# A hybrid decoder step with a 32-expert MoE: the experts' tokens picked out by one-hot products instead of indirect DMA

## What is computed

```python
h = _rmsnorm(x, norm_ffn)                       # 320 rows of 1024
logits = h @ w_router + b_router                # 32 experts
top_v, top_e = lax.top_k(logits, 4); gate = softmax(top_v)
# for each expert e, with the rows xe of h that chose it:
gu = xe @ w_gu[e] + b_gu[e]                     # 1024 x 2048
gt, up = jnp.split(gu, 2, axis=-1)              # clamped at 7
act = gt * sigmoid(1.702 * gt) * (up + 1.0)
out = act @ w_dn[e] + b_dn[e]                   # 1024 x 1024
# y[token] = sum over its four experts of gate * out
```

## Time and profile before

| | before |
|---|---|
| median of 3 runs | 1393.08 us (1392.92 to 1396.97) |
| the profiled execution, its own time | 1394.72 us |
| span in the profile | 1393.0 us |
| PE busy | 1274.7 us (92%) |
| DVE, ACT, POOL busy | 446.9, 238.9, 113.2 us |
| moved by DMA | 480.87 MB |

### The profile page before, as it was taken

How to read it: one execution, slowest core, us unless ns; L and a number is a source line. 1 busy time by engine, 2 the same in 40 slices (tenths; PEclk the granted TensorE clock), 3 DMA queues, 4 the chain that set the end, 5 groups by cost and what they waited for, 6 DMA issues and landing times.

```text
span 1393.0 us, 14359 instructions
## 1 busy us (share of the span) xinstructions
PE 1274.7 (92%) x5899; PEld 578.1 (41%) x5899; DVE 446.9 (32%) x793; ACT 238.9 (17%) x343; POOL 113.2 (8%) x140
## 2 busy tenths in 40 slices
PE   6999899999999999999999999999988877778881
PEld 5665677676463333333333333333332222223220
DVE  1697211121265331312222223322242222332216
ACT  3201343330121110111111111101121111111101
POOL 0110100000000100001100100001101100000100
PEclk9999999999999999999999999999999999999995
DMA  9614602734779999999999999999999999999994
GB/s 338 235 61 141 246 1 86 277 110 193 286 283 395 421 425 425 426 426 427 424 426 426 427 424 425 426 427 425 423 427 426 425 424 425 426 426 425 426 374 152
DMA packets 63366, 480.87 MB, mean 345 GB/s; under 512 B 11831, under 2 KB 11959, under 8 KB 38569
## 3 DMA queue, kind: packets, MB, share of 16 engines
q1 hardware_dynamic: 51327, 464.60, 80.8%
q0 software_dynamic: 9584, 10.37, 2.1%
q10 hardware_dynamic: 2362, 4.56, 0.9%
HBM read 479.83 MB, written 22.35 MB: 361 GB/s over the span
## 4 chain that ended last, share of the span: by engine, by line
PE 72%; DMA 24%; DVE 1%; ACT 1%; issue 1%; SPq 0%; POOL 0%; POOLq 0%; DVEq 0%
PE PS L1629 28%; PE PS L1290 15%; PE PS L1660 14%; DMA XX<-in_w_dn 12%; DMA XX<-in_w_gu 9%; PE PS L1236 4%; PE PS L1450 4%; PE PS L1492 3%; PE PS L1314 2%; DMA arena<-y_rows 1%; DMA ring<-in_w_in 1%; DMA arena<-h_rows,arena 1%; DMA y_rows<-arena 1%; PE PS L1368 0%; PE PS L1535 0%
## 5 line engine op out<-in xcount | busy, mean ns | idle before, releaser
L1629 PE MATMUL PS<-ring,arena 128*64 128x512 f32 x1840 | 412.3, 599 | 30.5 <-DMA ring<-in_w_gu 25.4
L1151 DVE TENSOR_TENSOR arena<-PS,XX 128x1024 f32<-128x1024 f32 x32 | 39.2, 1225 | 656.4 <-PE PS L1629 656.4
L1629 PEld LDWEIGHTS PS<-ring,arena 128*64 128x64 f32 x1840 | 130.5, 138 | 287.2 <-issue 285.2
L1290 PE MATMUL PS<-arena,ring 128*128 128x320 f32 x768 | 214.7, 437 | 3.1 <-DMA ring<-in_w_in 3.1
L1290 PEld LDWEIGHTS PS<-arena,ring 128*128 128x128 f32 x768 | 145.8, 192 | 63.7 <-issue 7.0
L1660 PE MATMUL PS<-ring,arena 128*64 128x512 f32 x656 | 148.2, 602 | 11.1 <-DMA ring<-in_w_dn 9.0
L790 ACT ACTIVATE arena<-arena 128x1024 f32<-128x1024 f32 x32 | 33.8, 1058 | 625.2 <-DVE arena L1154 625.1
L521 POOL DMA_INDIRECT y_rows<-arena x64 | 63.9, 998 | 823.9 <-ACT arena L781 814.1
L1629 PE MATMUL PS<-arena 128*64 128x512 f32 x432 | 97.7, 603 | 11.0 <-DMA arena<-in_w_gu 11.0
L1660 PE MATMUL PS<-arena 128*64 128x512 f32 x384 | 85.3, 596 | 5.3 <-DMA arena<-in_w_dn 5.3
L1236 PEld LDWEIGHTS PS<-ident,arena 128*128 128x128 f32 (+4 forms) x596 | 65.4, 143 | 58.5 <-issue 48.4
(11 more groups left out here) (190 smaller groups left out, 757.5 us busy)
## 6 DMA issues: line engine op xcount, KB each, us to landing
ring<-in_w_gu SPq DMA_DIRECT2D x95, 2048.0 KB, 29.5
ring<-in_w_dn SPq DMA_DIRECT2D x33, 2048.0 KB, 31.6
arena<-in_w_gu SPq DMA_DIRECT2D x22, 2048.0 KB, 29.4
arena<-in_w_dn SPq DMA_DIRECT2D x20, 2048.0 KB, 28.5
ring<-in_w_in SPq DMA_DIRECT2D x12, 2048.0 KB, 12.2
XX<-in_w_dn SPq DMA_DIRECT2D x11, 2048.0 KB
XX<-in_w_gu SPq DMA_DIRECT2D x10, 2048.0 KB
ring<-in_w_mem_kv SPq DMA_DIRECT2D x2, 2048.0 KB, 20.1
```

The costliest lines, as they stand in the source:

```text
L1151: nc.vector.tensor_tensor(gbuf[:], PS[:, 0:2, :], g_bias, ALU.add).then_inc(main["g_added"], 1)
L1290: last = mm(PS[:, j % 2, 0:T], w[:, k, m * P:(m + 1) * P], hT[:, k, :], start=k == 0, stop=k == KT - 1)
L1629: last = mm(PS[64 * h:64 * h + 64, 2 * g + b, :], tokens[:, k, :], (spare[kk] if m == BONUS else moe_ring(m, 2)[:, kk]) [:, g * D + h * 51 ...
```

## The change

The indirect fetch is gone: no `h_rows`, no `gather`, no `TG`, no `XG`. For every expert DVE's new `take` makes a one-hot `taken` (three row tiles x 128 slots, two buffers in turn) by comparing `R` with a row of numbers, `iota_s` or, for odd experts, the reversed `iota_b`, as `order` did for expert 0 alone. PE's new `take_tokens` stands where `turn_tokens` stood and multiplies it with `XN` in SBUF, as `first_tokens` did: 8 x 3 products instead of 8 transposes. The table has one column per expert. `XN` now has to stay whole through the loop, so `spread` (the bias rows by `stream_shuffle`, now two instructions of 512 columns), the gates `GD` and the loads of `b_dn` leave it, and `XX` is one row tile larger with `low` for small things. `turn_gates`, the copy `GT` and the two `b_dn` loads move behind the loop. The pieces of the diff below come in the order SP, POOL, ACT, DVE, PE, behind the one on the places in SBUF.

```diff
-    XX = sb("XX", [P, 2 * TT, D])
-    X, XN = XX[:, 0:TT, :], XX[:, TT:2 * TT, :]
+    XX = sb("XX", [P, 2 * TT + 1, D])
+    low, X, XN = XX[:, 0, :], XX[:, 1:TT + 1, :], XX[:, TT + 1:2 * TT + 1, :]
...
-    entries = view(16352, TT, TOPK, 2, NE)
+    entries = view(16352, TT, TOPK, NE)
-    XG = [view(15328, D), view(18400, D)]
+    taken = view(15328, 2, TT, WIN)
-    spread = XN[:, 2, :].rearrange("p (g n) -> p g n", g=2)
+    spread = [view(14816, 512), view(18400, 512)]
...
     # SP, ahead of the first load into LATE
                 sp.wait_ge(x_kept, 48)
-                sp.wait_ge(h_out, 48)
                 sp.wait_ge(main["xt_turned"], 1)
...
     # POOL
         def window(v):
-            pool.wait_ge(main["tg_ready"], v + 1)
-            if v:
-                gather(v, 0)
-            gather(v, 1)
             pool.wait_ge(main["zi_ready"], v + 1)
-            for e in range(2, NE):
-                gather(v, e)
-                if e >= 3:
-                    scatter(v, e - 3)
-            for e in range(NE - 3, NE):
+            for e in range(NE):
                 scatter(v, e)
...
     # ACT
         def keep_rows(tt):
-            rows = h_rows[tt * P:tt * P + ROWS[tt], :]
-            act.dma_start(rows, XN[0:ROWS[tt], tt, :]).then_inc(h_out, 16)
             act.dma_start(x_keep[tt * P:tt * P + ROWS[tt], :], X[0:ROWS[tt], tt, :]).then_inc(x_kept, 16)
...
-        for h in range(2):
-            act.dma_start(bdn[NE * h:NE * (h + 1), :], a["b_dn"][0][:, 512 * h:512 * (h + 1)]).then_inc(bdn_in, 16)
         act.wait_ge(cnt_ready, 1)
         most = act.value_load(maxi[0:1, 0:1], min_val=0, max_val=T)
         window(0)
...
+        act.wait_ge(gt_done, 1)
+        for h in range(2):
+            act.dma_start(bdn[NE * h:NE * (h + 1), :], a["b_dn"][0][:, 512 * h:512 * (h + 1)]).then_inc(bdn_in, 16)
+        nc.scalar.activation(GT[0:2 * NE, :], PS[0:2 * NE, 7, 0:T], ACT.Copy).then_inc(gt_ready, 1)
...
     # DVE
+        def take(v, e):
+            if NE * v + e > 1:
+                dve.wait_ge(main["xt_turned"], NE * v + e - 1)
+            for tt in range(TT):
+                r = ROWS[tt]
+                last = nc.vector.tensor_scalar(taken[0:r, e % 2, tt, :], (iota_b if e % 2 else iota_s)[0:r, :],
+                                               1024.0 + 512.0 * e + WIN * v, R[0:r, tt, e:e + 1], ALU.add, ALU.is_equal)
+            last.then_inc(main["taken_ready"], 1)
+
         fetch_list(0)
+        take(0, 1)
...
             for e in range(NE):
                 n = NE * v + e + 1
-                nc.vector.stream_shuffle(spread, bias[:], mask=[e] * 32).then_inc(main["spread_ready"], 1)
+                for g in range(2):
+                    last = nc.vector.stream_shuffle(spread[g], bias[:, g, :],
+                                                    mask=[e] * 32)
+                last.then_inc(main["spread_ready"], 1)
...
                     .then_inc(main["act_ready"], 1)
+                if e + 2 < NE:
+                    take(v, e + 2)
...
     # PE
-        def turn_tokens(v, e):
-            pe.wait_ge(main[f"gathered{e % 2}"], 16 * ((NE // 2) * v + e // 2 + e % 2))
-            rows = XG[e % 2]
-            if NE * v + max(e - 1, 0):
+        def take_tokens(v, e):
+            n = NE * v + e
+            pe.wait_ge(main["taken_ready"], n)
+            if n > 1:
                 pe.wait_ge(main["actT_ready"], NE * v + max(e - 1, 0))
+
             for k in range(KT):
-                last = tr(PS[:, 6 + k // 4, (k % 4) * WIN:(k % 4 + 1) * WIN], rows[:, k * P:(k + 1) * P])
+                for tt in range(TT):
+                    r = ROWS[tt]
+                    last = mm(PS[:, 6 + k // 4, (k % 4) * WIN:(k % 4 + 1) * WIN], XN[0:r, tt, k * P:(k + 1) * P],
+                              taken[0:r, e % 2, tt, :], start=tt == 0 and k % 4 == 0, stop=tt == TT - 1 and k % 4 == 3)
             last.then_inc(main["xt_turned"], 1)
```

More of the change, by code:

```diff
@@ L264, in program @@
     first_done, wr_ready = sem("first_done"), sem("wr_ready")
-    nffn_in, bias_in, h_out = (sem(s) for s in ("nffn_in", "bias_in", "h_out"))
+    nffn_in, bias_in = (sem(s) for s in ("nffn_in", "bias_in"))
     gates_ready, summed, x_kept, x_back = (sem(s) for s in ("gates_ready", "summed", "x_kept", "x_back"))
@@ L270, in program @@
     fin_in, fin_out = sem("fin_in"), sem("fin_out")
-    names = ("chunk_used", "spread_ready", "g_added", "u_clipped", "gathered0", "gathered1", "xt_turned", "xT_half", "xT_ready", "gu_done", "g_ready", "gu_read", "sig_done",
+    names = ("chunk_used", "spread_ready", "g_added", "u_clipped", "taken_ready", "xt_turned", "xT_half", "xT_ready", "gu_done", "g_ready", "gu_read", "sig_done",
              "prod", "act_ready", "ta_done", "actT_ready", "dn_done", "zs_ready", "scattered",
-             "shifted", "listed", "table_done", "tg_ready", "dest_ready", "moved", "zi_ready")
+             "shifted", "listed", "table_done", "dest_ready", "moved", "zi_ready")
     main = {s: sem(s) for s in names}
     bonus_in = sem("bonus_in")
-    h_rows = nc.dram_tensor("h_rows", (T, D), F32, kind="Internal").ap()
     x_keep = nc.dram_tensor("x_keep", (T, D), F32, kind="Internal").ap()
@@ L1135, in _ @@
             nc.vector.tensor_scalar(gates[0:r, tt, :], gsel[0:r, tt, :], gden[0:r, tt:tt + 1], None, ALU.mult)
-            if tt == 0:
-                dve.wait_ge(h_out, 48)
-                dve.wait_ge(main["xt_turned"], 1)
             for h in range(2):
@@ L1144, in window @@
         def window(v):
+            if v:
+                take(v, 0)
+                take(v, 1)
             for e in range(NE):
                 n = NE * v + e + 1
-                nc.vector.stream_shuffle(spread, bias[:], mask=[e] * 32).then_inc(main["spread_ready"], 1)
+                for g in range(2):
+                    last = nc.vector.stream_shuffle(spread[g], bias[:, g, :],
+                                                    mask=[e] * 32)
+                last.then_inc(main["spread_ready"], 1)
                 dve.wait_ge(main["spread_ready"], n)
                 dve.wait_ge(main["gu_done"], n)
-                g_bias, u_bias = (spread[:, i:i + 1, :].to_broadcast([P, 2, 512]) for i in range(2))
+                g_bias, u_bias = (spread[i][:, None, :].to_broadcast([P, 2, 512]) for i in range(2))
                 nc.vector.tensor_tensor(gbuf[:], PS[:, 0:2, :], g_bias, ALU.add).then_inc(main["g_added"], 1)
@@ L1549, in table_part @@
             for j in range(TOPK):
-                last = mm(PS[:, 7, 0:2 * NE], slots[0:r, tt, j, :], entries[0:r, tt, j].rearrange("p x e -> p (x e)"),
+                last = mm(PS[:, 7, 0:NE], slots[0:r, tt, j, :], entries[0:r, tt, j, :],
                           start=tt == 0 and j == 0, stop=tt == TT - 1 and j == TOPK - 1)
@@ L1694, in window @@
             if v:
-                turn_tokens(v, 0)
+                take_tokens(v, 0)
             for e in range(NE):
@@ L1706, in window @@
                 if e + 1 < NE:
-                    turn_tokens(v, e + 1)
-                elif v == 0:
-                    turn_gates()
+                    take_tokens(v, e + 1)
                 if e:
@@ L1714, in window @@
                     down(v, e - 1)
-                if v == 0 and e == NE - 1:
-                    pe.wait_ge(gt_ready, 1)
                 if e:
@@ L1742, in _ @@
         pe.nop()
+        turn_gates()
         for tt in range(TT):
```

46 lines of the change are left out of this document (13 added, 33 removed).

## The result

| | before | after |
|---|---|---|
| median | 1393.0 us (4 runs) | 1540.47 us (4 runs, 1539.65 to 1541.42) |
| ratio to before | | 1.1046, 95% interval 1.1032 to 1.106 |
| span in the profile | 1393.0 us | 1537.9 us |
| PE busy | 1274.7 us (92%) | 1490.6 us (97%) |
| moved by DMA | 480.87 MB | 474.60 MB |

147 us slower, where 71 were forecast, and far outside the range. The direction and the bound came out as written, and every term within 3 us but one, the price of the products.

What follows compares the result with a forecast made beforehand. Before, the weight stream bounds the experts, with PE equally full early; after, PE bounds the loop. Net PE work 153.2 less 79.1 idle gives +74.1, clock -1, end -2: +71 us, 1465.7 profiled, 1464 median; range 1450 to 1478.

Steps and rivals of the forecast that it cites:

- The price of the products: PE in the loop: 48 records at 0.125 us, 6.0 us an expert (5.9 to 6.2), net 4.98, in 31 turns 154.4 us.
- The idle time and the bound: PE behind expert 21: all 79.1 us of idle time are filled and PE becomes the bound of the whole loop.
- a lead that runs out: Weight ring behind the last expert with two blocks: its lead just lasts or falls short, adding 0 to 5 us.
- The first fetch: PE before expert 1's tokens: the wait of 1.19 us for the indirect DMA goes, gain 1.2 us.
- DMA: Weight stream: dropped fetches are worth 12 us to a stream that bounds, nothing to one that waits for PE.
- DVE: DVE in each turn: three comparisons, 0.7 to 0.9 us, and a bias spread in two parts, all hidden.
- The end: Behind the loop: between -4.3 and +2 us, taken as -2, and -1 for the clock in expert 31's `down`.
- rival 1: Loop behind expert 21: products hide in PE's idle time and the lighter stream makes it faster, 1381 us; 3%.
- Rival 2: Products in the loop: cheaper between long streams, 0.1 us a record, but not hidden, 1437 us; 6%.
- C: Follow-up theory on the products: records are slow because of the long streams around them, whatever their order; 8.4 us, 1540 us.
- Rival 3: Products in the loop: each costs four transposes, 12.3 us an expert, 1659 us; 1%.
- Rival 4: PE in each turn: a new wait for DVE or ACT, or a lower clock, 0.5 us a turn, 1480 us; 8%.

## Why the prediction was wrong, point by point

- **The price of the products: this is the step that failed.** "I take 0.125: 6.0 us an expert, bounds 5.9 and 6.2." It measured 8.45. Two things lay behind it. The 0.125 was a group's span divided by its count, and so held the 0.19 us of the group's edges and, in the 24, one change of height; the pace itself is 0.112. And `first_tokens` has the row tile outermost, which I named as the same shape without looking at the order in which the shapes follow each other. The two errors have opposite signs: without changes of height an expert would be 5.55, the fifteen changes make it 8.45. The bounds came from two rows of one and the same order, so they couldn't bound it.
- **The idle time and the bound: right.** Every microsecond of it filled, PE busy throughout, no wait on a chunk in the loop. With 8.45 in the place of 6.0 the working gives 1420.5 + 76.0 = 1496.5 for the turn of expert 31's activations; it is at 1496.80. The few microseconds for a lead that runs out were nothing at this price; with the row tile outermost and 5.75 us, where PE's own work alone would end at 1412.7, the turn is at 1420.63, so there they were 8.
- **The first fetch: right.** The products start behind `move_dest` with no wait, at 430.13 where the transposes started at 431.16:

```profile
429.56 0.64 PE L1544 MATMUL PS<-arena,ident 128*64 128x16 f32 x16
430.13 4.18 PE L1587 MATMUL PS<-arena,XX 128*128 128x128 f32 x23
```

- **DMA: right**, 11 us in a stream that binds, nothing here.
- **DVE: right.** The three comparisons take 0.66 us, behind the last step of an expert, and 22 us of waiting for gate/up follow:

```profile
522.44 0.66 DVE L1100 TENSOR_SCALAR arena<-iota_b,arena 128x128 f32<-128x128 f32 x3
...
545.97 1.23 DVE L1134 TENSOR_TENSOR arena<-PS,arena 128x1024 f32<-128x1024 f32 x1 [21.59 <-PE PS L1617]
```

- **The end: -5.5 us, -3 forecast.** The cause was the one named, result rows that no longer queue behind weights. The first of them were asked for at 1343.76 in before and at 1494.70 in after, and VectorE had them 23.3 us later there, 12.3 here, in before behind the end of `down`, here ahead of it:

```profile
1367.10 3.67 DVE L1217 SCALAR_TENSOR_TENSOR ring<-ring,arena 128x1024 f32<-128x1024 f32 x3 [23.37 <-DMA ring<-y_rows]
```

```profile
1506.98 3.67 DVE L1201 SCALAR_TENSOR_TENSOR ring<-ring,arena 128x1024 f32<-128x1024 f32 x3 [10.23 <-DMA ring<-y_rows]
```

The clock was not: `down` of expert 31 took 8.78 us again. The terms behind `down`, put at 17.9 us, add up to 17.6; nothing hangs on it.
- **Rivals.** The gain of rival 1 exists, 11 us, where PE's work hides: its threshold of 2.55 us an expert took all turns as equal and lies too high: at 2.75 it allows for 31 x 0.2 = 6 us, and the turn came 33 late. Rival 2 and C named the surroundings; they are worth the 0.19 us at the edges of a group, which `first_tokens` had too, and don't touch the pace. Rival 3's factor of four is off, the factor of two was right: read from start to start, a transpose is 0.109 us (its 1.02 / 8 = 0.128 holds the group's edges), a product of two records 0.224. Rival 4 did not come.
- **The range** held part of a new wait and small errors of the end; it stopped at 1478, 2 us short of the forecast's own upper end. Nothing in it stood for a spacing that depends on the neighbour.

## What to carry over

A matmul's price is the distance from start to start, and it belongs to a pair of neighbours, not to a shape. When a group is priced from other rows, compare the order of the shapes in both, and take the pace from the record starts, without the group's edges. Keep tiles of one height together in the inner loop, or pad the short one; both are free here and worth 70 to 75 us.

In a stream with a ring, idle time has a place. Extra work hides only in the stretch where the engine waits, so a trade of bandwidth for work is made for those turns and not for all.

## What the runs showed of the hardware

- Float32 records with a stationary operand of 128 or 64 rows x 128 columns and 128 columns moving follow each other every 0.112 us, weight loads included; a change between 128 and 64 rows adds 0.19 us, in both directions, and so does a change between 64 and 128 stationary columns at the edges of a group. With 32 columns moving the spacing is 0.112 as well, and 0.058 if the stationary operand has 64 columns; the change between these two adds 0.115.
- At such a change the weight load starts with its product; without one it starts 0.11 us ahead of it (0.03 with 32 columns moving).
- Transposes of 128 x 128 in float32 follow each other every 0.109 us, against 0.224 for a product of two records.
- `down` of expert 31 does not always run at the upper of the clock's levels (2.4 GHz; the lower is 1.2). Its 32 records as stretches of the changed kernel and of the one with the gates put back (columns as in the earlier trace rows; the granted clock is the third number from the end):

```profile
1499.90:1508.70 8.80, 8.78 (x32) 2.60 (x32) 1.72 (x2) 0.00 (x0) 0.71 (x1) 0.81 1.03 307
```

```profile
1501.90:1509.00 7.10, 7.06 (x32) 2.21 (x32) 0.00 (x0) 0.00 (x0) 0.97 (x1) 1.00 1.04 350
```

8.78 us at a mean clock of 0.81, or 7.06 at 1.00, both behind a full loop and a wait of 2.0 us for the activations. In the first the granted clock is 0.57 up to 1503.7 and 0.99 from there on. The changed kernel has one wait more, 0.28 us ahead of the transposes; whether that decides between them, no run shows.
